# A streaming encoder step: the sample projected inside chunk 0, kept in DRAM, and finished during the last chunk in buffers of its own

## What is computed

```
h = rmsnorm(x, norm_g);  u = h @ w_in            # 11 splits of 256 columns
a_b, a_c, a_x, a_g, b_v, b_a, b_g, c_u, c_g, x_q, x_g = split(u, 11)
A: y_a = a_b * conv3(hist_a | a_c*a_x) * silu(a_g)
B: y_b = silu(layernorm(conv31(hist_b | b_v*sigmoid(b_a)))) * silu(b_g)
C: y_c = (pool_w(trailing means over 2,4,8,16 of (hist_p | c_u) - c_u) + pool_bias) * pool_scale * silu(c_g)
X: y_x = attention(x_q, mem_k, mem_v; 4 heads, 256 memory tokens) * silu(x_g)
y = rmsnorm(x + concat(y_a, y_b, y_c, y_x) @ w_out, final_norm_g)
```

## Time and profile before

| | us |
|---|---|
| median of 3 runs | 1483.63 (1483.12 to 1484.98) |
| the profiled execution | 1483.44 |
| its span in the trace | 1481.7 |
| busy: TensorE / VectorE / ScalarE / GpSimd | 1431.8 / 1178.6 / 563.4 / 217.9 |

### The profile page before, as it was taken

One profiled execution on the slowest core, in us unless ns is written; L12 is line 12 of the kernel. 1 busy time (PEld: TensorE's weight loads), 2 busy tenths in 40 slices (PEclk: granted clock), 3 DMA queues, 4 the chain that ended last, 5 costly groups with the idle time before them and its releaser, 6 DMA issues.

```text
span 1481.7 us, 32647 instructions
## 1 busy us (share of the span) xinstructions
PE 1431.8 (97%) x11758; PEld 1226.0 (83%) x11758; DVE 1178.6 (80%) x3088; ACT 563.4 (38%) x1238; POOL 217.9 (15%) x180
## 2 busy tenths in 40 slices
PE   5978999999999999999999999999999999999996
PEld 4757888888888888888888888888888888888884
DVE  6997795969789595968869596987959697896965
ACT  6774332433333343423423243333324333332323
POOL 0161110111111011111110111111101111110110
PEclk9989999999999999999999999999999999999998
DMA  9986546455644635565463545555464556446374
GB/s 268 260 300 226 186 115 227 155 184 198 226 173 130 248 120 207 178 219 191 158 246 93 216 170 201 198 195 202 113 235 147 184 198 227 177 136 236 121 245 164
DMA packets 128386, 284.16 MB, mean 192 GB/s; under 512 B 12393, under 2 KB 69405, under 8 KB 128349
## 3 DMA queue, kind: packets, MB, share of 16 engines
q1 hardware_dynamic: 128349, 283.68, 55.7%
HBM read 225.60 MB, written 58.03 MB: 191 GB/s over the span
## 4 chain that ended last, share of the span: by engine, by line
PE 90%; DVE 4%; DMA 2%; issue 1%; ACT 1%; POOL 0%; SPq 0%; ACTq 0%; DVEq 0%
PE u L529 21%; PE u L530 20%; PE u L531 20%; PE sps L529 5%; PE sps L531 4%; PE sps L530 4%; PE qps L529 4%; PE qps L531 4%; PE qps L530 4%; PE ops L610 2%; DMA ring<-wo_split 1%; PE sps L741 1%; DVE z L1392 1%; DVE w_hl L1374 1%; DVE prow L1416 0%
## 5 line engine op out<-in xcount | busy, mean ns | idle before, releaser
L529 PE MATMUL u<-h_hi,w_hl 128*128 128x256 f16 (+1 forms) x2992 | 789.1, 269 | 12.4 <-DVE w_hl L1374 10.2
L530 PE MATMUL u<-h_lo,w_hl 128*128 128x256 f16 (+1 forms) x2992 | 788.1, 269 | 0.0
L531 PE MATMUL u<-h_hi,w_hl 128*128 128x256 f16 (+1 forms) x2992 | 787.9, 269 | 0.0
L1392 DVE SCALAR_TENSOR_TENSOR z<-glu,cst,z 128x256 f32<-128x256 f32 (+1 forms) x1020 | 424.1, 486 | 0.5
L529 PEld LDWEIGHTS u<-h_hi,w_hl 128*128 128x128 f16 x2992 | 293.0, 98 | 58.0 <-issue 12.0
L531 PEld LDWEIGHTS u<-h_hi,w_hl 128*128 128x128 f16 x2992 | 293.0, 98 | 32.9
L530 PEld LDWEIGHTS u<-h_lo,w_hl 128*128 128x128 f16 x2992 | 293.0, 98 | 32.7 <-issue 0.7
L894 ACT ACTIVATE gate<-u,inv 128x256 f32<-128x256 f32 (+1 forms) x204 | 82.7, 456 | 122.1 <-PE u L531 121.9
L1838 POOL TENSOR_TENSOR sa<-cu 128x540 f32<-128x540 f32 (+1 forms) x17 | 30.6, 1802 | 562.8 <-ACT cu L894 499.1
L529 PE MATMUL sps<-ring,y_hi 128*128 128x512 f32 (+1 forms) x262 | 104.1, 397 | 0.1
L529 PE MATMUL qps<-ring,y_hi 128*128 128x512 f32 x258 | 102.6, 398 | 1.4 <-DMA ring<-wo_split 1.4
(11 more groups left out here) (226 smaller groups left out, 1851.3 us busy)
## 6 DMA issues: line engine op xcount, KB each, us to landing
ring<-wo_split SPq DMA_DIRECT2D x256, 512.0 KB, 7.7
ob<-in_x_prompt SPq DMA_DIRECT2D x34, 512.0 KB, 4.1
probs_turned<-probs SPq DMA_DIRECT2D x130, 128.0 KB, 2.4
pt<-probs_turned SPq DMA_DIRECT2D x32, 512.0 KB, 3.5
out<-ob SPq DMA_DIRECT2D x32, 512.0 KB, 3.5
rows_turned<-rows SPq DMA_DIRECT2D x114, 128.0 KB, 2.4
w_hl<-in_w_in SPq DMA_DIRECT2D x20, 512.0 KB, 7.3
wo_split<-ring SPq DMA_DIRECT2D x16, 512.0 KB, 4.9
```

What stands on the lines that cost most here:

```text
L529: nc.tensor.matmul(out, a_hi, b_hi, start=first, stop=False)
L530: nc.tensor.matmul(out, a_hi, b_lo, start=False, stop=False)
L531: return nc.tensor.matmul(out, a_lo, b_hi, start=False, stop=last)
L1392: ins = nc.vector.scalar_tensor_tensor(z[:, c, 0:n], glu[:, c, k:k + n], w, z[:, c, 0:n], ALU.mult, ALU.add)
```

## The change

- The sample's rows are loaded into `xb` at the start. Their squares are taken on ScalarE (`sample_squares`), their norm is made together with that of the two tiles of memory rows (`memory_rms`, three columns at once, in place of two single ones), ScalarE scales them, GpSimd multiplies by the gain (`sample_gain`), TensorE transposes them into `ops`, ScalarE and VectorE make high and low parts in `hs`.
- `sample_project(g)` makes the sample's 11 projections in chunk 0, between the steps of the first chunk on TensorE, into the two banks of `qps`. `raw_keep` copies them to SBUF, `raw_leaves` stores them to DRAM (`sample_raw`), and `raw_returns` brings them back in the last chunk, into the weight memory of splits that are used up by then.
- Every buffer of the sample (tuple S, `work(i)`) lies in `w_hl` too, so its steps are written between those of the last chunk on all engines. Its scores go to `qps`, its mix and attention to the bank U[2], at the sample's slots.
- The sample's first eight output pieces are the ones in `late` now (loaded when x_g of the last chunk is projected, before the ring pieces 8 to 15 of that chunk); its last eight are the ring's pieces of the last chunk, which stay there (`sample_pieces`).
- Removed are the loading, norm, turning and splitting of the sample's rows in the last chunk. The load of the first rows of chunk 1 into `xb` waits for the sample's transposes.

The diff, cut to the order of the queues (removed lines of the orders are left out; S.x is a buffer of the sample). ScalarE's order of the last chunk is interleaved in the same way as VectorE's; only the part at `value_squares(1)` is shown:

```diff
+RAW_BANKS = ((0, 4), (4, 8), (8, 11))
...
-            late = [w_late[:, b % 2, b // 2] for b in range(RING)]
+            late = [w_late[:, b % 2, 7 + b // 2] for b in range(RING)]
...
+            def raw_returns(k):
+                a, m = ((0, 1024), (1024, 384))[k]
+                sp.wait_ge(u_ready.sem, slot(LAST, ORDER[(0, 6)[k]])[0])
+                sp.dma_start(raw_at[k], sample_raw[:, a:a + m]).then_inc(raw_back.sem, 16)
...
+                for k in range(3):
+                    sp.wait_ge(raw_out[k].sem, 16)
+                raw_returns(0)
                 sp.dma_start(st_rows[0:HB, 0:GW], state_conv_b[0, 0]).then_inc(st_in.sem, 16)
                 sp.dma_start(st_rows[0:HP, GW:2 * GW], state_pool[0, 0]).then_inc(st_in.sem, 16)
                 sp.dma_start(st_rows[0:HA, 2 * GW:3 * GW], state_conv_a[0, 0]).then_inc(st_in.sem, 16)
...
+                sp.wait_ge(u_ready.sem, slot(LAST, "x_q")[0])
+                for src, off in ((cache_mem_k, 0), (cache_mem_v, GW)):
+                    sp.dma_start(kv_s[:, :, off:off + GW], src[0, 0].rearrange("(t p) h d -> p t (h d)", p=P)).then_inc(kv_in.sem, 16)
+                probs_across(LAST, 0, N)
+                raw_returns(1)
+                sp.dma_start(xs, x_sample[0]).then_inc(res_s.sem, 16)
+                probs_across(LAST, 1, N)
+                probs_across(CHUNKS, 0, SAMPLE)
+                sp.wait_ge(u_ready.sem, slot(LAST, "x_g")[0])
+                for b in range(RING):
+                    sp.dma_start(late[b].bitcast(F32), wo_split[b]).then_inc(wo_late.sem, 16)
+                for q in range(RING, PIECES):
                     ring_load(LAST, q)
...
                 project(0, N, "x_q")
+                sample_transposes()
...
                 weight_sums(6)
+                for g in range(3):
+                    sample_project(g)
                 memory_product(5)
                 project(0, N, "c_u")
                 memory_product(6)
                 weight_sums(7)
                 weight_sums(8)
                 memory_product(7)
+                sample_project(3)
                 project(0, N, "a_c")
...
                 scores(0, N, 1)
+                for g in range(4, 8):
+                    sample_project(g)
                 project(0, N, "b_g")
                 weight_sums(10)
+                sample_project(8)
                 project(0, N, "c_g")
                 attend(0, N, 0)
                 mix(0, N)
+                sample_project(9)
                 project(0, N, "x_g")
                 z_rows(0, N)
+                sample_project(10)
                 attend(0, N, 1)
...
             def last_chunks():
...
+                i, n = CHUNKS, SAMPLE
+                project(LAST, N, "b_a")
+                project(LAST, N, "b_v")
+                project(LAST, N, "x_q")
+                states_in()
+                project(LAST, N, "c_u")
+                scores(LAST, N, 0)
+                project(LAST, N, "a_c")
+                keys_t(1)
+                value_sum(1)
+                project(LAST, N, "a_x")
+                scores(LAST, N, 1)
+                project(LAST, N, "a_b")
+                for p in range(PAIRS):
+                    scores(i, n, p)
+                project(LAST, N, "a_g")
+                attend(LAST, N, 0)
+                mix(LAST, N)
+                project(LAST, N, "b_g")
+                project(LAST, N, "c_g")
+                attend(LAST, N, 1)
+                project(LAST, N, "x_g")
+                z_rows(LAST, N)
                 out_begin(LAST, N)
...
+                out_pieces(LAST, N, 0, Z_AT)
                 z_back(LAST, N)
...
+                out_pieces(LAST, N, Z_AT, 10)
+                mix(i, n)
                 for p in range(PAIRS):
...
+                    attend(i, n, p)
+                out_pieces(LAST, N, 10, PIECES)
                 states_out(0, N)
...
+                z_rows(i, n)
+                sample_pieces(0, 6)
                 states_out(1, SAMPLE)
...
+                sample_pieces(6, 10)
+                z_back(i, n)
+                sample_pieces(10, PIECES)
...
+                exps(LAST, N, 0)
+                probs_hi(LAST, N, 0)
+                act.wait_ge(u_ready.sem, slot(LAST, "c_u")[0])
+                scaled_out(i, n, "x_q", S.dq_hi, ACT.Copy, q_hi)
+                cu_out(i, n)
                 value_squares(1)
+                scaled_out(LAST, N, "a_c", gate[:, 1, :, 0:N], ACT.Copy, ac_ok)
+                scaled_out(i, n, "a_c", S.gate[:, 1], ACT.Copy, ac_ok)
...
+            def last_chunks():
                 i, n = CHUNKS, SAMPLE
...
+                histories(LAST)
+                normalise(LAST - 1, N)
+                glu_out(LAST, N)
+                taps_free(LAST)
+                taps(LAST, N, 0, 6)
+                q_low(LAST, N)
+                taps(LAST, N, 6, 10)
                 histories_in()
                 glu_out(i, n)
...
+                taps(LAST, N, 10, 11)
+                softmax_max(LAST, N, 0)
+                taps(LAST, N, 11, 12)
+                softmax_rcp(LAST, N, 0)
+                taps(LAST, N, 12, 14)
+                probs_lo(LAST, N, 0)
                 q_low(i, n)
...
+                taps(LAST, N, 14, 15)
+                pool_diff(LAST, N)
+                value_scale(1)
+                keys_lo(1)
+                taps(LAST, N, 15, 17)
+                va_out(LAST, N)
+                softmax_max(LAST, N, 1)
+                conv_a_taps(LAST, N)
+                d_low(LAST, N)
+                values_lo(1)
+                ab_out(LAST, N)
+                softmax_rcp(LAST, N, 1)
                 softmax_max(i, n, 0)
+                taps(LAST, N, 17, 19)
+                probs_lo(LAST, N, 1)
+                softmax_rcp(i, n, 0)
+                taps(LAST, N, 19, 23)
+                probs_lo(i, n, 0)
+                taps(LAST, N, 23, TB)
+                ya_out(LAST, N)
                 pool_diff(i, n)
...
                 va_out(i, n)
...
                 conv_a_taps(i, n)
                 ab_out(i, n)
...
+                taps_free(i)
+                taps(i, n, 0, 6)
+                z_stats(LAST, N)
+                yx_out(LAST, N)
+                z_norm(LAST, N)
+                d_low(i, n)
                 ya_out(i, n)
+                taps(i, n, 6, 12)
+                yb_out(LAST, N)
+                taps(i, n, 12, 28)
+                yx_out(i, n)
+                taps(i, n, 28, TB)
+                add_half(LAST, N, 0)
+                add_half(LAST, N, 1)
                 z_stats(i, n)
                 z_norm(i, n)
...
+                out_root(LAST, N)
                 yb_out(i, n)
...
+                out_scale(LAST, N)
                 add_half(i, n, 0)
                 add_half(i, n, 1)
                 normalise(i, n)
...
+            def sample_gain():
+                pool.wait_ge(xs_step.sem, XS_SCALED)
+                pool.wait_ge(gx_ok.sem, 4)
+                nc.gpsimd.tensor_tensor(xb[0:SAMPLE, :], xb[0:SAMPLE, :], gx[0:SAMPLE, :], ALU.mult).then_inc(xs_step.sem, 1)
```

More of the change, by code:

```diff
@@ L13 @@
+from collections import namedtuple
 from contextlib import ExitStack
@@ L184, in encoder_program, with work @@
+        def work(i):
+            return S if type(i) is int and i == CHUNKS else C
         U = [ctx.enter_context(nc.psum_tensor(f"u{b}", [P, HALF], F32)) for b in range(3)]
@@ L282, in emptied @@
                 name, j = FIRST[n], 0
+            elif type(i) is int and i == CHUNKS:
+                name, j = {"mix": ("x_g", LAST), "zf": ("zf", LAST), "zb": ("zf", CHUNKS)}[name]
             else:
@@ L410, in probs_leave @@
                 sp.wait_ge(p_t_ok.sem, p_t_ok.at(i, p + 1))
-                put_out(probs_turned[p], turned_p, min(n, P), probs_out[p])
+                last = type(i) is int and i == CHUNKS
+                put_out(probs_turned[PAIRS if last else p], work(i).turned_p, min(n, P), probs_out[p])
             def probs_arrive(i, p, n):
@@ L895, in scaled_out, with squares @@
                 ins.then_inc(s.sem, 1)
-            def squares(j, t, m, i=0, rows=xb, loaded=None):
+            def squares(j, t, m, i=0, rows=xb, loaded=None, into=X_SQ):
                 if loaded:
@@ L1107, in first_chunk @@
                 w_high(2)
-                squares(2, 0, P, rows=ob[:, 0], loaded=first_in[2].sem)
-                squares(3, 1, P, rows=ob[:, 1], loaded=first_in[3].sem)
+                sample_squares()
+                squares(2, 0, P, rows=ob[:, 0], loaded=first_in[2].sem, into=M_SQ)
+                squares(3, 1, P, rows=ob[:, 1], loaded=first_in[3].sem, into=M_SQ)
                 w_high(3)
@@ L1242, in last_chunks @@
[L1242 to L1252 removed]
+                y_high(i, n, 0, S.ya, ya_ok)
@@ L1459, in pool_diff @@
                 dve.wait_ge(win_ok.sem, win_ok.at(i, 4))
-                if needed(yc_ok.at(i, 0)):
+                b = work(i)
+                if needed(yc_ok.at(i, 0)) and b is C:
                     dve.wait_ge(yc_ok.sem, yc_ok.at(i, 0))
```

569 lines of the change are left out of this document (353 added, 216 removed).

## The result

The changed kernel takes 1493.15 us (median of 5 runs, 1491.39 to 1493.85) against 1483.98 us for the kernel before on the same chip (5 runs): ratio 1.0059, 95% interval 1.0045 to 1.0072. The forecast was 1471.7. The change costs 9 us where it was to save 12. Two of the six runs of e11 (1843.20 and 5788.08 us) are slow ones and are left out of all that follows. The profiled execution took 1493.85 us, its span is 1492.0.

A forecast was written before the change was run, and what follows sets the result against it. TensorE, busy 97% of the span, was taken as the bound. Tail saved 18.7 us (1463.0), chunk 0 added 6.8 (span 1469.8), plus 1.74 outside the span and 0.19 to the median: 1471.7 us, range 1465 to 1479.

The forecast's parts named there:

- what stays on TensorE: Last chunk: the sample's transposes, value sum, scores, mix and attends cost 3.6 us, no cheaper than before; only waits go.
- (d): Last chunk, late loads before ring pieces 8 to 15: piece 8 lands 1427.7, wanted 1428.6; hidden, bounds 0 to 4 us.
- four waits that were named: New last-chunk waits: value_sum 1.9 us, taps nothing, third pair of pieces 2.9 us, ring piece 8 hidden.
- Projection out of the tail: The sample's 528 matmuls of 64 columns, 11 groups of 1.5 us, leave the tail: 16.5 us.
- the tail behind the last chunk's pieces, 22.5: From the last full-width piece to the span's end: 22.5 us instead of 42.
- (a): Last chunk, TensorE's value_sum(1) before a_x waits for ScalarE's squares of cached values: 1.9 us, bounds 0 to 3.
- (c): Last chunk, yx_out behind sample work on VectorE, slowed by GpSimd: TensorE waits 2.9 us for pieces 4, 5; bounds 0 and 4.
- (b): Last chunk, VectorE's taps end 1409.6 instead of 1402.8, TensorE wants them 1413.2: 3.6 us of cover, no cost.
- Rival 4: VectorE becomes the last chunk's bound: handoff waits of 23 us pass the cover, 1491 us; chance 0.07, 0.05 of it slower.
- Chunk 0, 6.8 us: Projection groups and transposes added to chunk 0's TensorE work cost 6.8 us, bounds 3 and 17.
- together about 3, under 5.1: Chunk 0: VectorE's lateness from the other new operations, about 3 us, lies under the 5.1 us shift from groups and transposes.
- What would show it: Signs: chunk 1 near 160.6, 6.62 us wait gone, 85.2 us a chunk, waits before a_x and third piece pair, tail 22.5.

The follow-up runs named there:

- e11: e9 with SP's ring loads 8 to 15 of the last chunk issued before the eight late loads; 1471.8 us, ratio 0.991.
- e8: e7 with last-chunk moves: VectorE's z_stats, yx_out, z_norm and out_scale before sample work, ScalarE's value_squares(1) before probs_hi; 1473.34 us, ratio 0.9917.
- e9: e8 with VectorE's last-chunk yb_out after three sample taps and ScalarE's sample probs_hi behind a_g; 1471.15 us, ratio 0.9889.
- e10: e9 with sample rows' load and squares behind the memory rows' in chunk 0, scale and gain in one VectorE operation; 1473.02 us, ratio 0.9896.
- e5: Changed kernel with one matmul per column group in the sample's projection (22 of 528), sample results left out; 1489.40 us in one run.
- e12: e10 with SP's ring loads 8 to 15 of the last chunk before the eight late loads; 1474.55 us, ratio 0.9929.
- e4: Changed kernel with states, cached keys and values loaded before the ring loads, and chunk 0's sample groups moved into TensorE's waits; 1477.62 us, ratio 0.9952.
- e7: e4 with the first raw-projection return and states' loads moved before the previous chunk's output-row stores; 1471.77 us, ratio 0.990.
- e1: Changed kernel with the first raw-projection return and three states' loads issued before the last chunk's eight ring loads; 1481.52 us, ratio 0.9974.
- e6: Changed kernel with four of the last chunk's eight ring loads before the states' loads and four behind; 1489.87 us in one run.

## Why the prediction was wrong

*The step that failed* is the sentence on what stays on TensorE: "They are no cheaper than before; only their waits go." For the state transposes it counted 0.5 us of work and no wait. In the kernel before, the states were issued from 1403.83 on, 38 us behind the last chunk's first eight ring loads (the last of them issued by 1365.6); the change puts their loads behind row stores, residual and ring, and their consumer ahead of c_u. The prediction followed SP's queue past the late loads (d) and past the stores of chunk 0, never past `residual(LAST)` and `ring_load(LAST, 0..7)`, though it had the price of a load (1.28 us). By that price eight ring loads need 10.2 us; SP issues the first 13.1 us after the last chunk's start (1371.04; in the kernel before 13.9), and TensorE asks 15.9 us after it (1373.9). So the ring loads alone are not through before 23 us, and a wait of 7 us or more could have been summed. Two loads of rows and the raw projections, 0.5 MB each, stand ahead of the states as well. The missing wait, with the slow matmuls behind it, was worth 16.8 us, more than all four waits that were named.

*Projection out of the tail, 16.5, and the tail behind the last chunk's pieces, 22.5.* Right. From the last full-width piece to the end it is 23.05 us (before: 42).

*The waits (a) and (c)* were 1.39 and 2.95 us (forecast 1.9 and 2.9), each with the releaser named. GpSimd's part in (c) is there too: the sample's `va_out` on VectorE takes 2.51 us beside two GpSimd operations, 0.48 in the earlier trace rows.

*(b) VectorE's taps, cover 3.6.* Right: ya_out follows the last tap at 1437.71 and z_rows starts at 1441.31, without a wait. Rival 4 was wrong; that its 1491 us lie near the measured time is chance.

*(d) late loads ahead of the ring loads.* Hidden, as forecast, but by less than the 0.9 us that were summed. In e8, e9 and e10 piece 8 can start 15.1, 14.9 and 15.0 us after the first late load is issued; in the changed kernel TensorE comes to it after 15.1 us, and 2.95 of these are wait (c). The forecast had 14.5 for the landing.

*Chunk 0, 6.8 us* (bounds 3 and 17): 10.4. The groups cost 5.5 by e5, where 6.2 of the 6.8 were theirs, so that term was right. The mis-sized term is the rest, dismissed with "together about 3, under 5.1": it took the larger of two delays where they add up. TensorE's third weight sum, in the kernel before and in the changed one:

```profile
24.42 0.59 PE L550 MATMUL u<-w_sq,ones 128*128 128x2 f32 x2 [3.56 <-ACT gate L951]
```

```profile
24.98 0.59 PE L630 MATMUL u<-w_sq,ones 128*128 128x2 f32 x2 [4.23 <-ACT gate L1114]
```

Already here, before any group, 0.6 us are lost, in e10 nothing (24.39); by the last memory product it is 3.3 us without a group (66.84 against 63.52 in the kernel before). The new front gives about 1 us of that back (65.48 in e10 and 65.86 in e12, where e4, e7, e8, e9 and e11 have 66.4 to 67.0). What the rest of the 4.9 us is made of was not tested apart.

*Of the 17.8 us behind the last chunk's start* some 1.0 is left after wait and clock. Half of it lies behind the last full-width piece (23.05 for 22.5); the rest is made of small differences that I can't assign.

*What would show it.* Most of the signs came out: the wait of 6.62 us is gone, the waits (a) and (c) are there, z_rows is free, the steady chunks and the tail are near the forecast. Chunk 1 is late, by 3.6 us. The list of what would prove the forecast wrong named VectorE, the ring loads and chunk 1, and no input of the sample.

## What to carry to other kernels

When work is moved earlier, list for each moved consumer the DMAs that feed it, and walk the issuing queue from the last wait ahead of them: its waits, then some 1.3 us for each half megabyte already queued (1.2 to 1.55 here). A small load behind large ones is as late as they are, and it is enough to issue it first. The place for moved matmuls is the idle time itself: the same eleven groups cost 5.5 us ahead of a busy chain and next to nothing (0.5) in the waits behind it.

Taking one wait away tells whether the next is hidden behind it: (c) covered the ring load. Moving that load ahead held up the late loads. Here everything that paid is in e7 (0.990): in the traces e9 and e10 are 2.2 and 3.7 us shorter behind the last chunk's start, but no median of e8 to e12 is under e7's by more than the intervals allow.

## What the runs showed that I had not expected

A short wait can cost more than its length. Behind waits of 3.3, 9.5 and 14.3 us c_u's 48 matmuls took 7.08, 7.83 and 7.95 us, behind none 5.41; behind the 1.4 us at `value_sum` the next 48 took 5.40. So 3.3 us idle cost 5.0.

The length alone doesn't decide it. Wait (c) is 2.9 to 3.0 us in the changed kernel and in e1 to e7; the two pieces behind it take 3.2 us in the changed kernel, e5 and e6, and 4.8 in e1 to e4 and e7. The wait in front of piece 8 is 1.97 us in e10 and 1.91 in e9; the two pieces behind it take 4.0 and 5.6 us. The granted clock goes with it (third from the right in the sums by stretch): 1.00, so 2.4 GHz throughout, where the pieces are quick, and a mean of 0.66 or 0.67, so 1.2 GHz for a part, where they are slow. The changed kernel and e7, behind (c):

```profile
1450.00:1454.00 4.00, 3.64 (x18) 3.05 (x19) 3.96 (x22) 0.14 (x1) 0.31 (x1) 1.00 1.02 412
```

```profile
1429.00:1434.00 5.00, 4.89 (x17) 3.90 (x17) 4.96 (x28) 0.00 (x0) 0.06 (x1) 0.66 1.02 414
```

e10 and e9, behind the wait for piece 8:

```profile
1436.00:1441.00 5.00, 4.34 (x43) 3.75 (x44) 5.00 (x26) 0.46 (x2) 0.49 (x1) 1.00 1.03 412
```

```profile
1433.80:1439.00 5.20, 5.12 (x20) 4.19 (x20) 5.20 (x27) 0.11 (x1) 0.49 (x1) 0.67 1.03 410
```

The 1.5 us between the last parts of e9 (116.0) and e10 (114.5) are this and no gain of an edit. No run here tests what makes the difference between two equal waits.

The steady chunks are not equally long. A chunk takes 85.04 us when nothing waits, and in every kernel some take up to 1.8 us more: over the fourteen, 2.3 us in the kernel before, 3.2 in the changed one, 1.2 in e8, 9.3 in e10. The first of the fourteen is always among the longer ones, by 0.6 to 1.5 us. Where a wait shows, it is almost always in front of the first of the last two pieces. TensorE's timeline in a steady chunk, of the kernel before and of e10:

```profile
237.46 0.47 PE L529 MATMUL qps<-ring,y_hi 128*128 128x512 f32 x1 [1.13 <-DMA ring<-wo_split]
```

```profile
1011.75 0.47 PE L610 MATMUL qps<-ring,y_hi 128*128 128x512 f32 x1 [0.65 <-DMA ring<-wo_split]
```

A ring load just misses its piece there. That is up to 9 us in a profiled execution from code that none of the edits touches, more than most of the terms of the sum, so the parts of a span are to be compared, not only the spans. Why some executions have more of it was not tried.
